# Moving the weight slots to a pitch of 4160 bytes, and the large buffers behind the small tables to multiples of 64 bytes, in a float32r transformer layer

## The reference

```python
x = layer_norm(ALPHA * x + 0.5 * swiglu(x, gate0, up0, down0))       # 1024 -> 2816 -> 1024
x = layer_norm(ALPHA * x + hybrid_mixer(x, w_in, ...) )              # 8 attention heads of 64, 4 mLSTM heads of 128
x = layer_norm(ALPHA * x + memory_attention(x, mem, xq, xkv, xo))    # 4 heads of 256, 256 memory rows
x = layer_norm(ALPHA * x + 0.5 * swiglu(x, gate1, up1, down1))
```

## Time and profile before

| | us |
|---|---|
| median of 3 runs (1222.26 to 1222.57) | 1222.52 |
| the profiled execution | 1222.48 |
| its span, first to last instruction | 1220.6 |
| PE busy in the span | 1208.8 |
| DVE busy | 539.8 |
| ACT busy | 407.7 |
| mean granted TensorE clock | 0.996 |

### The profile page before, as it was taken

One profiled execution on the slowest core, in us unless ns is written; L12 is line 12 of the kernel. 1 busy time (PEld: TensorE's weight loads), 2 busy tenths in 40 slices (PEclk: granted clock), 3 DMA queues, 4 the chain that ended last, 5 costly groups with the idle time before them and its releaser, 6 DMA issues.

```text
span 1220.6 us, 14762 instructions
## 1 busy us (share of the span) xinstructions
PE 1208.8 (99%) x5532; PEld 968.8 (79%) x5532; DVE 539.8 (44%) x840; ACT 407.7 (33%) x666; POOL 31.2 (3%) x45
## 2 busy tenths in 40 slices
PE   9999999999999999999999999999999999999997
PEld 7888888888888677788788887778888888888886
DVE  3523333343337455644785743337333323243325
ACT  4312221233224444443354444434312212232322
POOL 2000000000001011010000000000000000000000
PEclk9999999999999999999989999999999999999999
DMA  8532323232212221142243261122322232232211
GB/s 291 180 103 88 101 86 103 87 115 92 91 66 102 70 78 52 45 155 69 87 138 97 94 207 52 52 85 89 121 93 96 86 103 86 99 107 99 91 35 69
DMA packets 33563, 120.85 MB, mean 99 GB/s; under 512 B 3900, under 2 KB 3916, under 8 KB 33264
## 3 DMA queue, kind: packets, MB, share of 16 engines
q1 hardware_dynamic: 30528, 109.07, 26.9%
q0 software_dynamic: 2992, 11.19, 2.6%
HBM read 118.13 MB, written 2.11 MB: 99 GB/s over the span
## 4 chain that ended last, share of the span: by engine, by line
PE 99%; ACT 1%; DVE 0%; issue 0%; DVEq 0%; POOL 0%; POOLq 0%; ACTq 0%
PE ps L392 30%; PE ps L394 29%; PE ps L393 29%; PE ps L580 2%; PE ps L603 2%; PE ps L803 1%; PE ps L793 1%; PE ps L681 1%; PE ps L409 1%; PE ps L590 1%; PE ps L665 1%; PE ps L532 0%; PE ps L618 0%; PE ps L775 0%; ACT ew L832 0%
## 5 line engine op out<-in xcount | busy, mean ns | idle before, releaser
L1222 DVE TENSOR_TENSOR wlo<-raw,whi 128x1024 fp32r<-128x1024 f32 x196 | 240.5, 1231 | 428.7 <-ACT whi L832 428.0
L392 PE MATMUL ps<-xth,whi 128*128 128x512 f32 (+1 forms) x928 | 365.8, 394 | 0.0
L394 PE MATMUL ps<-xth,wlo 128*128 128x512 f32 (+1 forms) x928 | 359.6, 388 | 0.0
L393 PE MATMUL ps<-xtl,whi 128*128 128x512 f32 (+1 forms) x928 | 359.6, 388 | 0.0
L832 ACT ACTIVATE whi<-raw 128x1024 fp32r<-128x1024 f32 (+1 forms) x204 | 206.8, 1036 | 158.7 <-PE ps L394 148.2
L394 PEld LDWEIGHTS ps<-xth,wlo 128*128 128x128 f32 x928 | 174.4, 188 | 39.3
L392 PEld LDWEIGHTS ps<-xth,whi 128*128 128x128 f32 x928 | 174.6, 188 | 38.7 <-issue 1.3
L393 PEld LDWEIGHTS ps<-xtl,whi 128*128 128x128 f32 x928 | 174.6, 188 | 38.6 <-issue 1.0
L392 PE MATMUL ps<-whi,hhi 128*128 128x512 f32 x480 | 192.1, 400 | 0.0
L393 PE MATMUL ps<-wlo,hhi 128*128 128x512 f32 x480 | 189.6, 395 | 0.0
L394 PE MATMUL ps<-whi,hlo 128*128 128x512 f32 x480 | 189.6, 395 | 0.0
(11 more groups left out here) (150 smaller groups left out, 933.6 us busy)
## 6 DMA issues: line engine op xcount, KB each, us to landing
raw<-in_units SPq DMA_DIRECT2D x204, 512.0 KB, 3.3
gb<-in_ln_g POOLq DMA_DIRECT2D x4, 512.0 KB, 3.8
gb<-in_ln_b POOLq DMA_DIRECT2D x4, 512.0 KB, 5.4
xn<-in_x POOLq DMA_DIRECT2D x4, 512.0 KB, 12.1
wb<-in_bias_by_key POOLq DMA_DIRECT2D x8, 256.0 KB, 3.8
out<-xn SPq DMA_DIRECT2D x8, 256.0 KB, 2.1
gsp<-g_rows POOLq DMA_DIRECT2D x1, 1024.0 KB, 7.6
memn<-in_mem_cols POOLq DMA_DIRECT2D x1, 1024.0 KB, 5.1
```

Of the source, the lines that this page charges most:

```text
L392: mm(dst, lh, rh, start=start, stop=False)
L393: mm(dst, lh, rl, start=False, stop=False)
L394: return mm(dst, ll, rh, start=False, stop=stop)
L1222: v.tensor_tensor(wlo[c % SPL][:, :], raw[c % RAW][:, :], whi[c % SPL][:, :].bitcast(F32), ALU.subtract).then_inc(lo_done, 1)
```

## The change

The twelve weight slots get a pitch of 4160 bytes (4096 + 64) instead of 4096, and `gb_at`, where the large regions begin, is rounded up to a multiple of 64 bytes. No instruction is added, removed or moved in its engine's order; only addresses differ.

```diff
         xn = sb("xn", [P, NB, D])
-        whi = [sb(f"whi{s}", [P, D], F32R) for s in range(SPL)]
-        wlo = [sb(f"wlo{s}", [P, D], F32R) for s in range(SPL)]
+        slots = cursor[0]
+        whi = [at(f"whi{s}", [P, D], slots + s * 4160, F32R) for s in range(SPL)]
+        wlo = [at(f"wlo{s}", [P, D], slots + (SPL + s) * 4160, F32R) for s in range(SPL)]
+        cursor[0] += 2 * SPL * 4160
         raw = [sb(f"raw{s}", [P, D]) for s in range(RAW)]
...
-
+        cursor[0] += -cursor[0] % 64
         gb_at = cursor[0]
         gb = at("gb", [P, 2, D], gb_at)
         craw = [at(f"craw{s}", [P, S + CK - 1], gb_at + s * 2080) for s in range(2)]
```

## The result

The changed kernel takes 1213.82 us (median of 4 runs, 1213.29 to 1214.24) against 1222.39 for the kernel before (4 runs, 1219.61 to 1222.57): a ratio of 0.9935, 95% interval 0.9918 to 0.9952. That is 0.65% faster; I had forecast no change, 1220.6 to 1224.4 us.

What follows compares the result with a forecast made beforehand. PE was taken to bound the kernel, with 99% of the chain. From 1222.48 us for the profiled execution, + 0 - 0.03 + 0 gave 1222.45, forecast as 1222.5, no change, range 1220.6 to 1224.4 us.

Steps and rivals of the forecast that it cites:

- The reading of the bound: Whole kernel: PE is 99% of the chain, so addresses act only through its matmul rate or its few us of waiting.
- The 0.1 us that I bounded for ACT and DVE: At PE's waits for DVE: ACT and DVE operations ahead change them by 0.1 us at most either way, taken as 0.
- the mixed offsets: ACT and DVE operations mixing aligned and offset operands: may cost 12 to 17 ns on ACT, 7 on DVE per 512 elements.
- part 1: Large regions on multiples of 64: 0 for PE's matmuls, -0.03 us for ACT and DVE work behind the last matmul.
- rows 4: Up stage, profile before: moving operand off by 32, stationary aligned, 233.3 ns between starts; taken to show offsets cost nothing.
- rows 5: Down stage, profile before: moving operand aligned, stationary off, 233.4 ns between starts; taken to show offsets cost nothing.
- rows 6: Gate product, profile before: read as both operands off, stationary of 36 columns, 231.3 ns; would be slowest if offsets cost time.
- Part 2: Slot pitch of 4160, half the slots on odd multiples of 64: taken as 0, with 1.8 us on both sides.
- 96 past a multiple of 128 is free: Up and down stage reads at 96 past a multiple of 128 cost nothing, so 64 past should not either.
- The rival with both operands aligned: All 4416 matmuls lose their extra 20.0 ns only when both operands are on multiples of 64: 88 us, 1134 us; chance 0.04.
- The rival of the moving clock dip: 1.2 GHz dip behind PE's 1.3 and 1.6 us waits: gone, 1219.7 us, chance 0.04; a second dip, 1225.3, chance 0.01.

Runs made afterwards that it cites:

- the map: Kernel with PE alone, layer left out: fourteen float32r matmuls for each of 100 pairs of stationary and moving start addresses; 226.7 ns where starts are equal modulo 256.
- the regions alone: Against the kernel before, only the large regions move to multiples of 64 bytes, the slot pitch stays 4096: 1196.0 us, ratio 0.9778.
- both 32 bytes on: Against the kernel before, pitch 4096, slots and large regions both 32 bytes past a multiple of 64, equal modulo 256: 1195.18 us, ratio 0.9781.

## Why the prediction was wrong

**The reading of the bound held.** PE was 99% of the path, and nothing but its rate moved; its waits stayed at 1.6, 1.3 and 0.5 us. The 0.1 us that I bounded for ACT and DVE were nothing, and the mixed offsets that I read into 632 and 692 ns are refuted by the rows above.

**The step that failed is part 1**, "If an offset of the moving stream cost time, rows 4 would be slower than rows 5; if one of the stationary operand did, the other way round". That test covers costs that each operand has by itself. The cost lies in the pair. In rows 4 the moving start was 32 bytes below the stationary one modulo 256, in rows 5 32 above: two entries of the map that both read 233.4. Equal distances in three cases did not mean that addresses were irrelevant; all three were cases of the same kind. I also read rows 6 wrongly, as a case with both operands off. `wg_hi` and `wg_lo` are taken in slices of 36 columns, 144 bytes apart, so that by the layout the stationary starts run through all multiples of 16 modulo 256, among them 192, 0, 64 and 128, which are on multiples of 64. One of its 24 matmuls, the fifth slice of `wg_lo` at 96 like `xth`, even had equal starts, but a single one between others says nothing on a settled pace. Of the 4416 matmuls with a weight slot none had equal starts, and their distances in the kernel before could not show what such a pair does.

**Part 2** took the pitch at 0 between bounds of 1.8 us. With the regions where the change puts them (128 modulo 256), a pitch of 4160 leaves slots 0 and 4 of whi and slot 2 of wlo at that place and spreads the others over the other three. Measured, the pitch costs 17.8 us there (1213.82 - 1195.99, from two sets of runs whose kernels before agree within 0.3 us). My bound was one step of 0.83 ns on half of the matmuls; the slots stand 2.2 to 6.5 ns above the 226.7 of the regions alone. For the down stages the first map, entry by entry, gives 230.4 ns in the mean, and 230.4 was measured; for the up stages it gives 230.7 against 232.1, and single slots are off by up to 3 ns. That pairs off the equal place cost time is shown by the runs; how a stream of changing pairs adds up is not. My argument that "96 past a multiple of 128 is free" compared absolute places again.

**The rival with both operands aligned** had the mechanism nearest to the truth, at a chance of 0.04, and its size was off: 6.7 ns of the 20.0 go, not all, and what has to agree is the place modulo 256, not alignment to 64. I had called it unlikely that an offset on either side should cost the same to 0.1 ns; the map has 233.3 to 233.8 in 15 of the 32 entries shown. The 215.8 ns at N = 512 by the formula that the Trainium skill gives for the warm gap of an isolated matmul ("TensorE: Matmul & The Clock Gate", Back-to-back issue gap) are right on this chip for bfloat16, 215.9 here; float32r never came below 226.7 at 512 columns.

**The rival of the moving clock dip** turned out real and had the right price. Of 13 runs of the kernel before beside the first experiments, three took 1219.5 to 1219.6 us at a mean clock of 0.998 to 0.999, the others 1221.9 to 1223.2 at 0.996 to 0.998. I had written 1219.7 for a run without the dip. I had also called the dip stable against small shifts, and it isn't even from one run to the next. It isn't what the change does, though: the changed kernel keeps the dip. Its four runs have mean clocks of 0.996 and 0.997, and in the windows view of PE its stretch around the two waits shows a granted clock below 1:

```profile
606.00:614.00 8.00, 5.06 (x23) 0.68 0.19 66
```

Among two kernels of one pace the profiled executions fell on either side, 1194.6 us of span with the dip (the regions alone) and 1191.4 without (both 32 bytes on). One stretch of each in the windows view of PE, in this order:

```profile
600.00:606.00 6.00, 5.17 (x24) 0.50 0.00 0
```

```profile
600.00:606.00 6.00, 5.74 (x49) 1.00 0.00 0
```

The numerators and what follows them run at the 1.2 GHz level in the first and at 2.4 in the second, with the same waits.

## What to carry to other kernels

For float32r matmuls with 128 stationary and 512 moving columns, place the two operands at the same offset modulo 256 bytes (on a multiple of 32): it was worth 2.2% here, and no instruction changed. For other widths measure first, as the best place differs (with 96 stationary columns even between two runs). A single odd-sized table ahead of a region is enough to lose it, and so is a pitch that isn't a multiple of 256. Read the distance between starts, not the durations, and when a rate is constant in a kernel don't take that as proof that it can't change: ask first which combinations the layout never contains.

## What I had not expected of the hardware

The distance of float32r matmuls of 512 columns has a floor of 226.7 ns where bfloat16 has 215.9, and goes up to 235 with the starts of the operands in SBUF, periodic in 256 bytes. A stream can need up to nine matmuls to settle. With 256 moving columns equal starts are slightly the slower case (119.6 ns against 117.6 at 32 bytes). The clock dip behind two waits of PE of 1.3 and 1.6 us comes in some runs and not in others of the same kernel, and costs some 3 us.
